# One decoder layer on one core: the last pair's gate products of the pooling branch moved in front of the branch, and three output-projection units issued row by row

## The chip, the cores and the metric

The kernel runs on one core of a Trainium2 chip, as one launch. The time is device microseconds (us) from the launch's start to its end. Every change is judged by the median of several runs; one further execution is recorded by the profiler, and all rows come from such a recorded execution.

## The reference, cut to what matters

The program computes one layer of a decoder trunk for a prompt of 1024 tokens and for 8 samples of 8 new tokens with a paged key/value cache. The part that matters here is the end of the token mixer:

```
z      = h @ w_in                                  # h: 1088 tokens x 1024
p      = z[..., OFF_P:OFF_G]                       # 4 groups of 128 channels
pooled = trailing mean of p over 2/4/8/16 positions, minus p
pool_out = einsum('btgc,gcd->btgd', pooled, pool_w) * pool_scale
gates  = sigmoid(z[..., OFF_G:]).reshape(B, T, 3, 1024)
merged = gates[:, :, 0] * (att      @ w_br_attn)
       + gates[:, :, 1] * (conv_out @ w_br_conv)
       + gates[:, :, 2] * (pool_out @ w_br_pool)
out    = merged @ w_o
x      = layer_norm(ALPHA * x + g1 * out, ln1_g, ln1_b)   # then SwiGLU and a second norm
```

Everything is float32 and has to be accurate, so each product is made of three: every operand is split into a high part that TensorE takes as it is and a low rest, and high*high, low*high and high*low are summed.

## The kernel before, in words

**Layout.** Activations lie transposed: 128 channels on the partitions, T = 1092 tokens (1024 prompt, 64 sample, 4 padding) along the row. `hhi` and `hlo` are the eight channel tiles of the mixer's input h, `ahi`/`alo` the four tiles of a branch's input, `merged` the eight tiles of the gated sum. CH = 364 is a third of T, one PSUM bank.

**Weights** come in 140 units of 128 rows x 1024 floats (one unit holds the group map, half that size). SyncE loads unit u into `raw[u % 3]` (L405); GpSimd splits it by a cast (L611) and a subtraction (L612) into `whi`/`wlo[u % 3]`. GpSimd may begin with unit u once TensorE has begun unit u-2 (semaphore `w_begun`). For the output projection the functions at L698 and L699 do the same into places of their own (`wohi`, `wolo`), so that all eight units stay; the units from the fourth on wait until the last branch product is done.

**TensorE** does a unit as one `gemm` (L1672, L1676, L1678): for each of eight weight blocks three thirds by three products, 72 matmuls of 364 columns. `psA` and `psB` hold three banks each and are used in turn (`GP`). The part that the change touches runs in this order:

- *Pooling filter.* Four units (`U_POOL`) give p of group 3, 2, 1, 0 (`POOL_ORDER`, windows 16, 8, 4, 2). For each, ScalarE copies PSUM to `pb` (L996), TensorE transposes the last 15 and the 64 sample tokens of `pb` for the state outputs (L2012, L2013), VectorE runs the window sums and subtracts (L1414 to L1429, into `yp`), ScalarE casts `yp` to `ahi` (L998), VectorE takes the rest into `alo` (L1433), ScalarE copies the transposed tokens to `ptok` and sends them out (L1002 to L1006).
- *Group maps.* One half unit: per group 9 matmuls. ScalarE scales into `ahi` (L1009), VectorE takes the rest into `alo` (L1437).
- *Third branch,* `branch(2, ...)`: a loop of four turns, one for each pair of channel tiles. A turn is a gate unit into psA, a gate unit into psB (ScalarE takes their sigmoids into `sg`, L967) and a branch unit, half of it into psA, half into psB. VectorE multiplies by the sigmoid (L1343) and adds into `merged` (L1345). The last pair's VectorE work stands apart (L1449 to L1457).
- *Low parts of merged.* ScalarE casts `merged` tile by tile to `hhi` (L1018, the eighth tile in two pieces at L1021), VectorE subtracts into `hlo` (L1444). In VectorE's order tiles 0 to 5 stand ahead of the last pair's product.
- *Output projection.* `wo(c, k)`: column piece c (428, 300 and 364 tokens) of output tile k: eight rows j of three matmuls (L2038, L2041, L2042), each waiting, for the very first, on `hlo` of tile j. The first three use the three banks of psA, the next three those of psB. VectorE's first eviction (L1476) needs the residual x, which ScalarE fetches into `merged` when all of `hlo` is done (L1025) and scales (L1028).

Each engine's program is written out by hand in the order in which it runs; waits on semaphores join them. Nothing is reordered by a scheduler.

Of the kernel before, what the change touches and what calls it, by code (L numbers as in the profile page):

```python
# [25 lines left out]
ALU = mybir.AluOpType  # L26
ACT = mybir.ActivationFunctionType

P = 128
D = 1024  # L30
KD = D // P
# [36 lines left out]
U_F, U_QKV, U_BRA, U_CONV, U_BRC, U_POOL, U_BRP, U_WO, U_FF0, U_FF, U_FFE, U_END = (  # L68
    0, 1, 13, 25, 37, 49, 54, 66, 74, 78, 138, 140)
RING = 3  # L70
# [28 lines left out]
def build(nc, a, out):  # L99
    with ExitStack() as ctx:  # L100
# [8 lines left out]
        class Region:  # L109
# [3 lines left out]
            def __call__(self, name, shape, dt=F32):  # L113
# [101 lines left out]
        S = Region(r_s, r_end - r_s)  # L215
        sg = [S("sg0", [P, T]), S("sg1", [P, T])]
        part = [S("part0", [P, T]), S("part1", [P, T])]

# [20 lines left out]
        s64 = S("s64", [P, 2, NS])  # L239
        S = Region(r_s + 4 * (4 * T + 16), 8 * 8 * P)  # L240
# [154 lines left out]
        def _(sp):  # L395
# [100 lines left out]

            def branch_loads(u0, gate, w, first=0):
                with sp.Fori(first, 4) as i:
# [14 lines left out]
            for j, g in enumerate(POOL_ORDER):  # L513
                wunit(U_POOL + j, (U_POOL + j) % RING, tiles(w_in, OFF_P + g * P))
            sp.wait_ge(s["w_split"], U_POOL + 4 - RING + 1)
            sp.dma_start(raw[(U_POOL + 4) % RING][:, 0:NT, :],
                         a["pool_w"][0].rearrange("g c d -> c g d")).then_inc(raw_in[(U_POOL + 4) % RING], 16)
            branch_loads(U_BRP, 2, a["w_br_pool"][0])
            for j in range(KD):
# [48 lines left out]
        def _(pool):  # L568
# [188 lines left out]
        def _(act):  # L757
# [204 lines left out]
            def gates(j):  # L962
                with act.Fori(0, 4) as i:
                    for x, ps in (("A", psA), ("B", psB)):
                        act.wait_ge(s[f"g{x}"], i + (4 * j + 1))
# [24 lines left out]
            act.wait_ge(s["mB"], 8)  # L990
            for j, g in enumerate(POOL_ORDER):
                act.wait_ge(s["gemm_done"], 1 + j + 1)
                if j:
                    act.wait_ge(s["pf_done"], j)
                    act.wait_ge(s["pt2_tr"], j)
                nc.scalar.copy(c3(pb[:, LEAD:LEAD + T]), cols(GP[j % 2])).then_inc(s["pcopied"], 1)  # L996
                act.wait_ge(s["pf_done"], j + 1)
                nc.scalar.copy(ahi[:, g, :], yp[:, :]).then_inc(s["phi_done"], 1)  # L998
# [117 lines left out]
        def _(dve):  # L1116
# [331 lines left out]
            dve.wait_ge(s["bA"], 12)  # L1448
            link(V.tensor_tensor(c3(part[0][:, :]), cols(GP[0]), c3(sg[0][:, :]), ALU.mult))  # L1449
            V.tensor_tensor(merged[:, KD - 2, :], merged[:, KD - 2, :], part[0][:, :], ALU.add).then_inc(s["mA"], 1)  # L1450
            merged_low(KD - 2, slice(0, T), KD - 1)
            dve.wait_ge(s["bB"], 12)
            for n, (c0, c1) in enumerate(((0, 2), (2, 3))):
                at = slice(c0 * CH, c1 * CH)
                link(V.tensor_tensor(part[1][:, at].rearrange("p (c n) -> p c n", n=CH), psB[:, c0:c1, 0:CH],
                                     sg[1][:, at].rearrange("p (c n) -> p c n", n=CH), ALU.mult))
                V.tensor_tensor(merged[:, KD - 1, at], merged[:, KD - 1, at], part[1][:, at], ALU.add).then_inc(s["mB"], 1)  # L1457
# [199 lines left out]
        def _(pe):  # L1657
# [297 lines left out]
            def branch(j, u0, free_a, free_b, ready):  # L1955

                for first, last in ((0, 1), (1, 4)):
                    with pe.Fori(first, last) as i:
# [19 lines left out]
                        for k, x in enumerate("AB"):  # L1978
                            gemm((u0 + 2) % RING, GP[k], [(2 * t + k, t) for t in range(NT)], ahi, alo, done=s[f"b{x}"],
                                 begin=k == 0, free=((s[f"sg{x}"], i + (4 * j + 1)),))  # L1980
                        if j < 2:
# [18 lines left out]
            branch(1, U_BRC, (s["y_done"], NT), (s["u_done"], NT), ((s["clo_done"], NT),))  # L2000

            for g in range(NT):
# [12 lines left out]
            for j, g in enumerate(POOL_ORDER):  # L2015
                if j >= 2:
                    pe.wait_ge(s["mlo_done"], j - 1)
                pe.wait_ge(s["plo_done"], j + 1)
                gemm((U_POOL + NT) % RING, GP[j % 2], [(g, g)], ahi, alo, done=s["gemm_done"],
                     begin=j == 0)  # L2020
            branch(2, U_BRP, (s["mlo_done"], NT), (s["mlo_done"], NT), ((s["mlo_done"], NT),))

            def wo(c, k):

                n, o = c * KD + k, wo_bank(c * KD + k)
                hi, lo = wo_w[k]
                if c == 0:
                    unit(U_WO + k)
                if n < 6:
                    pe.wait_ge(s["mA" if n < 3 else "mB"], 12 if n < 3 else 13)  # L2030
                else:
                    pe.wait_ge(s["wo_ev"], n - 5 if n < 2 * KD + 6 else 2 * KD + 3 * (n - 5 - 2 * KD) - 1)
                if n == KD:
                    pe.wait_ge(s["hlo_done"], 2 * KD + 1)
                for j in range(KD):
                    if n == 0:
# [5 lines left out]
                    m = mm(o, lo[:, j, :], hhi[:, j, WCOL[c]], start=False, stop=j == KD - 1)  # L2042
                m.then_inc(s["gemm_done"], 1)

# [22 lines left out]

            for k in range(KD):
                wo(0, k)
# [152 lines left out]
```

## Time and profile before

| | |
|---|---|
| median of 3 runs | 2244.74 us (2244.55 to 2249.45) |
| the profiled execution, its own time | 2240.87 us |
| span of its instructions | 2239.3 us |
| granted TensorE clock, mean over the span | 0.966 |
| TensorE matmul busy | 2087.5 us (93%) |
| VectorE / ScalarE / GpSimd busy | 793.1 / 387.1 / 636.6 us |

Times inside the profile are microseconds from the start of the span. A row of the timeline gives the start, the length, the engine, the line of the kernel, the operation, the tiles that it writes and reads, and in square brackets how long the engine had stood idle before it and which instruction ended that. Where equal rows follow one another they are merged and counted (x3). The recorded length of a matmul reaches a little into the next one, so the distance from one start to the next is the better measure: 24 groups of three matmuls make up a unit.

### The profile page before, as it was taken

Reading aid. Unit: us, or ns where it says so; the run is one execution under the profiler, and the core shown is the slowest. Engines: PE = TensorE matmul, PEld = TensorE weight load, DVE = VectorE, ACT = ScalarE, POOL = GpSimd, SP = SyncE. Lnnn points to the kernel's source line nnn. Section 1 sums busy time; section 2 is a strip of 40 time slices with the busy share of each in tenths; the row PEclk is TensorE's granted clock in tenths of the full one; section 3 lists DMA queues with packets and bytes.
Section 4 is the critical chain, followed back from the end, with each engine's and each line's share of the span. In section 5 each row is a group of like instructions: output and inputs, shape, how many; then the busy total and the mean of one; then the engine's idle time right before and its main releaser. Section 6 shows DMA issues by size and latency. Waiting matters only on the chain.

```text
span 2239.3 us, 33058 instructions
## 1 busy us (share of the span) xinstructions
PE 2087.5 (93%) x13046; PEld 1966.5 (88%) x13046; DVE 793.1 (35%) x1423; ACT 387.1 (17%) x700; POOL 636.6 (28%) x482
## 2 busy tenths in 40 slices
PE   4989999788899999999879989899999999999996
PEld 3978887644599999999879989899999999999996
DVE  2444545543200132201622347532334224332326
ACT  2434444412110000000110114400000000000003
POOL 5031111042222322322223334423223323323323
PEclk8989998879999999999989999999999999999998
DMA  9321102067533112222111130011111111111112
GB/s 298 95 80 58 39 29 77 20 227 252 171 98 99 38 38 84 76 76 80 40 39 42 53 127 19 29 48 46 39 47 47 38 47 47 37 47 47 38 38 80
DMA packets 175713, 164.05 MB, mean 73 GB/s; under 512 B 15134, under 2 KB 139506, under 8 KB 175499
## 3 DMA queue, kind: packets, MB, share of 16 engines
q1 hardware_dynamic: 153307, 132.50, 19.3%
q0 software_dynamic: 6144, 17.01, 2.4%
q10 hardware_dynamic: 16184, 13.46, 2.0%
q8 instruction: 54, 0.88, 0.2%
q14 instruction: 24, 0.20, 0.0%
HBM read 149.03 MB, written 14.03 MB: 73 GB/s over the span
## 4 chain that ended last, share of the span: by engine, by line
PE 83%; DVE 7%; issue 2%; SPq 2%; ACT 2%; DMA 2%; POOL 1%; POOLq 0%; ACTq 0%; DVEq 0%
PE psA L1672 11%; PE psA L1678 10%; PE psA L1676 10%; PE psB L1678 9%; PE psB L1676 9%; PE psB L1672 9%; PE psB L1781 2%; PE psB L1784 2%; PE psB L1785 2%; PE psB L1940 2%; PE ps L1850 1%; PE ps L1906 1%; PE psA L1867 1%; DMA kpage<-in_cache_k 1%; DVE hlo L1444 1%
## 5 line engine op out<-in xcount | busy, mean ns | idle before, releaser
L611 POOL CAST whi<-raw 128x1024 fp32r<-128x1024 f32 x131 | 138.7, 1059 | 1208.3 <-PE psA L1672 621.8
L612 POOL TENSOR_TENSOR wlo<-raw,whi 128x1024 fp32r<-128x1024 f32 x131 | 321.3, 2453 | 10.5
L1672 PE MATMUL psA<-hhi,whi 128*128 128x364 f32 x1032 | 230.0, 331 | 11.6 <-DVE yc L1384 7.2
L1678 PE MATMUL psA<-hhi,wlo 128*128 128x364 f32 x1032 | 229.6, 331 | 0.0
L1676 PE MATMUL psA<-hlo,whi 128*128 128x364 f32 x1032 | 229.5, 331 | 0.0
L1678 PE MATMUL psB<-hhi,wlo 128*128 128x364 f32 x936 | 206.8, 329 | 0.0
L1676 PE MATMUL psB<-hlo,whi 128*128 128x364 f32 x936 | 206.7, 329 | 0.0
L1672 PE MATMUL psB<-hhi,whi 128*128 128x364 f32 x936 | 205.8, 328 | 0.0
L1672 PEld LDWEIGHTS psA<-hhi,whi 128*128 128x128 f32 x1032 | 179.8, 190 | 13.6 <-issue 13.5
L1678 PEld LDWEIGHTS psA<-hhi,wlo 128*128 128x128 f32 x1032 | 181.0, 190 | 0.0
L1676 PEld LDWEIGHTS psA<-hlo,whi 128*128 128x128 f32 x1032 | 180.6, 190 | 0.0
L1557 DVE TENSOR_TENSOR ft<-psB,sil 128x1092 f32<-128x1092 f32 x22 | 28.5, 1296 | 405.0 <-PE psB L1678 399.4
L1678 PEld LDWEIGHTS psB<-hhi,wlo 128*128 128x128 f32 x936 | 162.8, 188 | 0.0
L1672 PEld LDWEIGHTS psB<-hhi,whi 128*128 128x128 f32 x936 | 162.3, 188 | 0.0
L1676 PEld LDWEIGHTS psB<-hlo,whi 128*128 128x128 f32 x936 | 162.3, 188 | 0.0
L1083 ACT CAST ahi<-ft 128x1092 fp32r<-128x1092 f32 x22 | 24.3, 1106 | 463.4 <-PE psB L1678 312.5
L1672 PE MATMUL psA<-ahi,whi 128*128 128x364 f32 x366 | 82.4, 334 | 8.5 <-DVE alo L1437 8.5
L1678 PE MATMUL psA<-ahi,wlo 128*128 128x364 f32 x366 | 81.1, 330 | 0.0
L1672 PE MATMUL psB<-ahi,whi 128*128 128x364 f32 x366 | 81.1, 330 | 0.0
L1676 PE MATMUL psA<-alo,whi 128*128 128x364 f32 x366 | 81.1, 330 | 0.0
L1676 PE MATMUL psB<-alo,whi 128*128 128x364 f32 x366 | 81.0, 330 | 0.0
L1678 PE MATMUL psB<-ahi,wlo 128*128 128x364 f32 x366 | 80.8, 329 | 0.0
(412 smaller groups left out, 3665.9 us busy)
## 6 DMA issues: line engine op xcount, KB each, us to landing
raw<-in_w_in SPq DMA_DIRECT2D x53, 512.0 KB, 4.0
raw<-in_w_gate_up SPq DMA_DIRECT2D x44, 512.0 KB, 3.8
kpage<-in_cache_k SPq DMA_DIRECT2D x64, 256.0 KB, 3.7
vpage<-in_cache_v POOLq DMA_DIRECT2D x64, 256.0 KB, 3.9
ada_late<-in_ada_w SPq DMA_DIRECT2D x8, 2048.0 KB, 8.0
raw<-in_w_down SPq DMA_DIRECT2D x22, 512.0 KB, 3.6
ada<-in_ada_w SPq DMA_DIRECT2D x4, 2048.0 KB, 17.2
x_keep<-xt SPq DMA_DIRECT2D x1, 4368.0 KB, 13.8
```

What stands on the lines that cost most here:

```text
L611: link(nc.gpsimd.tensor_copy(whi[slot][:, 0:n, :], raw[slot][:, 0:n, :]))
L612: nc.gpsimd.tensor_tensor(wlo[slot][:, 0:n, :], raw[slot][:, 0:n, :], whi[slot][:, 0:n, :].bitcast(F32), ALU.subtract).then_inc(s["w_split ...
L1083: nc.scalar.copy(to, ft[k][:, :]).then_inc(s["fhi_done"], 1)
L1444: V.tensor_tensor(hlo[:, k, at], merged[:, k, at], hhi[:, k, at].bitcast(F32), ALU.subtract).then_inc(s["hlo_done"], 1)
L1557: V.tensor_tensor(c3(ft[k][:, :]), cols(psB), c3(sil[k][:, :]), ALU.mult).then_inc(s["ft_done"], 1)
L1672: m = mm(ps[:, c, 0:CH], whi[slot][:, b, :], hi[:, k, c * CH:(c + 1) * CH], start=first, stop=False)
L1676: mm(ps[:, c, 0:CH], whi[slot][:, b, :], lo[:, k, c * CH:(c + 1) * CH], start=False, stop=False)
L1678: m = mm(ps[:, c, 0:CH], wlo[slot][:, b, :], hi[:, k, c * CH:(c + 1) * CH], start=False, stop=last)
L1781: m = mm(bank[:, 0:CH], whi[slot][:, k, :], hhi[:, k, at], start=k == 0, stop=False)
L1784: mm(bank[:, 0:CH], whi[slot][:, k, :], hlo[:, k, at], start=False, stop=False)
L1785: m = mm(bank[:, 0:CH], wlo[slot][:, k, :], hhi[:, k, at], start=False, stop=k == KD - 1)
L1940: m = mm(psB[rows, 2, :], ptrs[:, g, rows], vpage[:, half * hpg + g, :], start=g == 0, stop=half == 0 and g == hpg - 1)
```

## The change

The gate units of the third branch's last pair (tiles 6 and 7) are taken out of the branch's loop and stand behind the four pooling units, ahead of the group maps. Their sigmoids go into two tiles of their own, `sgl`, which keep until the end. The loop has three turns, and the last pair's branch unit follows it alone, once the VectorE sums of the third turn have freed psA and psB. TensorE's transposes of one group's tokens, and ScalarE's copies and sends of them, move behind the next unit's product. The output projection's first three units (column piece 0) are issued row by row: rows 0 to 5 of all three, then row 6 of all three, then row 7. The loads and splits of the weight units follow the new order.

```diff
 U_F, U_QKV, U_BRA, U_CONV, U_BRC, U_POOL, U_BRP, U_WO, U_FF0, U_FF, U_FFE, U_END = (
-    0, 1, 13, 25, 37, 49, 54, 66, 74, 78, 138, 140)
+    0, 1, 13, 25, 37, 49, 56, 66, 74, 78, 138, 140)
...
+        S = Region(r_end - 8768, 8768)
+        sgl = [S("sgl0", [P, T]), S("sgl1", [P, T])]
...
+            for j in range(2):
+                wunit(U_POOL + 4 + j, (U_POOL + 4 + j) % RING, tiles(w_in, 3 * 256 + OFF_G + 2 * D + j * P))
+            sp.wait_ge(s["w_split"], U_POOL + 6 - RING + 1)
+            sp.dma_start(raw[(U_POOL + 6) % RING][:, 0:NT, :],
+                         a["pool_w"][0].rearrange("g c d -> c g d")).then_inc(raw_in[(U_POOL + 6) % RING], 16)
+            branch_loads(U_BRP, 2, a["w_br_pool"][0], last=3)
+            wunit(U_BRP + 9, (U_BRP + 9) % RING, tiles(a["w_br_pool"][0], 3 * 256, 256), 4)
...
-            for u_ in range(U_POOL, U_POOL + 4):
+            for u_ in range(U_POOL, U_POOL + 6):
                 one(u_)
-            one(U_POOL + 4, NT)
-            three(U_BRP, 4)
+            one(U_POOL + 6, NT)
+            three(U_BRP, 3)
+            one(U_BRP + 9)
...
             def gates(j):
-                with act.Fori(0, 4) as i:
+                early = j // 2
+                with act.Fori(0, 4 - early) as i:
...
+            for j, g in enumerate(POOL_ORDER):
+                act.wait_ge(s["gemm_done"], 1 + j + 1)
+                if j:
+                    act.wait_ge(s["pf_done"], j)
+                    act.wait_ge(s["pt2_tr"], j)
+                nc.scalar.copy(c3(pb[:, LEAD:LEAD + T]), cols(GP[j % 2])).then_inc(s["pcopied"], 1)
+                if j:
+                    last_rows(j - 1)
+                act.wait_ge(s["pf_done"], j + 1)
+                nc.scalar.copy(ahi[:, g, :], yp[:, :]).then_inc(s["phi_done"], 1)
+            for k, x in enumerate("AB"):
+                act.wait_ge(s[f"g{x}"], 9)
+                nc.scalar.activation(c3(sgl[k][:, :]), cols(GP[k]), ACT.Sigmoid).then_inc(s[f"sg{x}"], 1)
+                if k == 0:
+                    last_rows(NT - 1)
...
-            link(V.tensor_tensor(c3(part[0][:, :]), cols(GP[0]), c3(sg[0][:, :]), ALU.mult))
+            link(V.tensor_tensor(c3(part[0][:, :]), cols(GP[0]), c3(sgl[0][:, :]), ALU.mult))
...
                 gemm(u0 % RING, GP[g % 2], all_k, done=s["gemm_done"])
-                pe.wait_ge(s["pcopied"], g + 1)
                 if g:
-                    pe.wait_ge(s["pt2_copied"], g)
-                tr(mi[0][0:PST, 0:P], pb[:, LEAD + NP - PST:LEAD + NP], ident[:, :])
-                tr(mi[0][0:NS, P:2 * P], pb[:, LEAD + NP:LEAD + TU], ident[:, :]).then_inc(s["pt2_tr"], 1)
-            unit(U_POOL + NT)
+                    last_rows(g - 1)
+            for k, x in enumerate("AB"):
+                u0 = U_POOL + NT + k
+                unit(u0)
+                gemm(u0 % RING, GP[k], all_k, done=s[f"g{x}"], free=((s["pcopied"], NT - 1 + k),))
+                if k == 0:
+                    last_rows(NT - 1)
+            u0 = U_POOL + NT + 2
+            unit(u0)
             for j, g in enumerate(POOL_ORDER):
-                if j >= 2:
-                    pe.wait_ge(s["mlo_done"], j - 1)
+                pe.wait_ge(s["mlo_done"] if j >= 2 else s["sgB" if j else "sgA"], j - 1 if j >= 2 else 9)
                 pe.wait_ge(s["plo_done"], j + 1)
...
             branch(2, U_BRP, (s["mlo_done"], NT), (s["mlo_done"], NT), ((s["mlo_done"], NT),))
-
-            def wo(c, k):
+            unit(U_BRP + 9)
+            for k, x in enumerate("AB"):
+                gemm((U_BRP + 9) % RING, GP[k], [(2 * t + k, t) for t in range(NT)], ahi, alo, done=s[f"b{x}"],
+                     begin=k == 0, free=((s[f"m{x}"], 11),))
+
+            def wo(c, k, js=range(KD)):
...
-                for j in range(KD):
+                for j in js:
...
-            for k in range(KD):
+            for js in (range(KD - 2), range(KD - 2, KD - 1), range(KD - 1, KD)):
+                for k in range(3):
+                    wo(0, k, js)
+            for k in range(3, KD):
                 wo(0, k)
```

ScalarE in the pooling filter, before: from the copy of the first group (window 16) to that of the third.

```order
L996 COPY pb<-psA 128x1092
L998 CAST ahi<-yp 128x1092
L1002 COPY ptok<-ps 15x128
L1003 COPY ptok<-ps 64x128
L1005 DMA out_pool_prompt<-ptok 15x128
L1006 DMA out_pool_sample<-ptok 8x8x128
L996 COPY pb<-psB 128x1092
```

ScalarE, the same place now.

```order
L1017 COPY pb<-psA 128x1092
L1021 CAST ahi<-yp 128x1092
L1017 COPY pb<-psB 128x1092
L1006 COPY ptok<-ps 15x128
L1007 COPY ptok<-ps 64x128
L1009 DMA out_pool_prompt<-ptok 15x128
L1010 DMA out_pool_sample<-ptok 8x8x128
```

The copy that frees PSUM for TensorE stands ahead of the former group's token copies and sends; they stand behind it.

TensorE behind the first pooling unit, before (the last group of its matmuls, the two transposes, the next unit).

```order
L1678 MATMUL psA<-hhi,wlo_56 128x364 x3
L2012 MATMUL ps<-ident,pb 15x128
L2013 MATMUL ps<-ident,pb 64x128
L1672 MATMUL psB<-hhi,whi_54 128x364 x3
L1676 MATMUL psB<-hlo,whi_54 128x364 x3
```

TensorE at the end of the second of the two moved gate units (psB), now, with the first two group maps behind it.

```order
L1698 MATMUL psB<-hhi,wlo_55 128x364 x3
L1692 MATMUL psA<-ahi,whi_53 128x364 x3
L1696 MATMUL psA<-alo,whi_53 128x364 x3
L1698 MATMUL psA<-ahi,wlo_56 128x364 x3
L1692 MATMUL psB<-ahi,whi_53 128x364 x3
L1696 MATMUL psB<-alo,whi_53 128x364 x3
L1698 MATMUL psB<-ahi,wlo_56 128x364 x3
```

Before, each pooling unit was followed at once by transposes that read `pb`; now a whole unit lies between a copy to `pb` and its transposes, and two gate units lie between the pooling units and the group maps.

TensorE in the output projection, before: from row 7 of the first unit to row 0 of the second.

```order
L2038 MATMUL psA<-hhi,whi_52 128x428
L2041 MATMUL psA<-hlo,whi_52 128x428
L2042 MATMUL psA<-hhi,wlo_55 128x428
L2038 MATMUL psA<-hhi,whi_53 128x428
L2041 MATMUL psA<-hlo,whi_53 128x428
L2042 MATMUL psA<-hhi,wlo_56 128x428
```

TensorE, row 6 of the first three units, now (whi_52, whi_53 and wohi_165 are the high parts of unit 1, 2 and 3).

```order
L2074 MATMUL psA<-hhi,whi_52 128x428
L2077 MATMUL psA<-hlo,whi_52 128x428
L2078 MATMUL psA<-hhi,wlo_55 128x428
L2074 MATMUL psA<-hhi,whi_53 128x428
L2077 MATMUL psA<-hlo,whi_53 128x428
L2078 MATMUL psA<-hhi,wlo_56 128x428
L2074 MATMUL psA<-hhi,wohi_165 128x428
L2077 MATMUL psA<-hlo,wohi_165 128x428
L2078 MATMUL psA<-hhi,wolo_166 128x428
```

Row 6 of the first unit is followed by row 6 of the second and third, and before it stand 54 matmuls that need only rows 0 to 5.

## Rows read from the trace of the kernel before

**Rows 1.** The page: the chain that ended last, by engine.

```profile
PE 83%; DVE 7%; issue 2%; SPq 2%; ACT 2%; DMA 2%; POOL 1%; POOLq 0%; ACTq 0%; DVEq 0%
```

**Rows 2.** TensorE's waits, 1060 to 1330 us: released by, total us, times, longest.

```profile
PE psA L1672 <- DVE alo L1437: 11.3, 2, 8.5
PE ps L2012 <- ACT pb L996: 6.6, 4, 3.0
PE psA L2038 <- issue: 6.3, 1, 6.3
PE psA L2038 <- DVE hlo L1444: 4.0, 1, 4.0
```

**Rows 3.** TensorE's timeline from the first pooling unit to the third branch.

```profile
1062.51 0.74 PE L1672 MATMUL psA<-hhi,whi 128*128 128x364 f32 x3
...
1075.97 0.28 PE L2012 MATMUL ps<-ident,pb 128*15 128x128 f32 x1 [1.24 <-ACT pb L996]
...
1091.36 0.28 PE L2012 MATMUL ps<-ident,pb 128*15 128x128 f32 x1 [3.01 <-ACT pb L996]
...
1131.91 1.28 PE L1672 MATMUL psA<-ahi,whi 128*128 128x364 f32 x3 [8.54 <-DVE alo L1437]
...
1139.88 1.25 PE L1672 MATMUL psA<-hhi,whi 128*128 128x364 f32 x3 [2.74 <-DVE alo L1437]
```

**Rows 4.** Two stretches: length, then busy us of each engine, PEclk, DMA share.

```profile
1091.50:1096.00 4.50, 4.50 (x20) 4.50 (x19) 4.36 (x5) 0.00 (x0) 2.55 (x2) 0.62 0.01 1
1292.00:1296.50 4.50, 4.47 (x13) 4.20 (x14) 3.40 (x2) 1.07 (x1) 4.42 (x3) 0.50 0.41 117
```

**Rows 5.** ScalarE's timeline: the psA sigmoids of the third and fourth turn.

```profile
1225.67 1.08 ACT L967 ACTIVATE sg<-psA 128x1092 f32<-128x1092 f32 x1 [22.96 <-PE psA L1678]
...
1261.69 1.08 ACT L967 ACTIVATE sg<-psA 128x1092 f32<-128x1092 f32 x1 [22.96 <-PE psA L1678]
```

**Rows 6.** VectorE's and ScalarE's timelines: first filter's end, last group map's rounding.

```profile
1087.18 0.22 DVE L1429 SCALAR_TENSOR_TENSOR yp<-ps,ps 128x64 f32<-128x64 f32 x1
...
1137.17 1.17 ACT L1009 ACTIVATE ahi<-psB,vecs 128x1092 fp32r<-128x1092 f32 x1 [0.95 <-PE psB L1678]
...
1138.38 1.35 DVE L1437 SCALAR_TENSOR_TENSOR alo<-psB,vecs,ahi 128x1092 fp32r<-128x1092 f32 x1 [0.77 <-ACT ahi L1009]
```

**Rows 7.** TensorE's timeline: the branch's end and the output projection's first three units.

```profile
1285.04 0.66 PE L1678 MATMUL psB<-ahi,wlo 128*128 128x364 f32 x3
1292.03 0.70 PE L2038 MATMUL psA<-hhi,whi 128*128 128x428 f32 x1 [6.33 <-issue]
...
1302.53 0.46 PE L2038 MATMUL psA<-hhi,whi 128*128 128x428 f32 x1 [4.03 <-DVE hlo L1444]
...
1309.42 0.35 PE L2038 MATMUL psA<-hhi,wohi 128*128 128x428 f32 x1
...
1314.08 0.35 PE L2038 MATMUL psB<-hhi,whi 128*128 128x428 f32 x1
```

**Rows 8.** VectorE's timeline at the same place.

```profile
1251.16 3.52 DVE L1345 TENSOR_TENSOR merged<-merged,part 128x1092 f32 x1 [0.15 <-DVE part L1343]
1275.78 12.79 DVE L1444 TENSOR_TENSOR hlo<-merged,hhi 128x1092 fp32r<-128x1092 f32 x6 [21.10 <-ACT hhi L1018]
...
1300.73 4.37 DVE L1444 TENSOR_TENSOR hlo<-merged,hhi 128x728 fp32r<-128x728 f32 x2
```

**Rows 9.** GpSimd's timeline: splits of weight units, alone and beside VectorE.

```profile
1250.01 1.04 POOL L611 CAST whi<-raw 128x1024 fp32r<-128x1024 f32 x1 [8.55 <-PE psA L1672]
1251.14 2.39 POOL L612 TENSOR_TENSOR wlo<-raw,whi 128x1024 fp32r<-128x1024 f32 x1
...
1277.43 2.11 POOL L698 CAST wohi<-raw 128x1024 fp32r<-128x1024 f32 x1
1279.62 3.34 POOL L699 TENSOR_TENSOR wolo<-raw,wohi 128x1024 fp32r<-128x1024 f32 x1
```

**Rows 10.** ScalarE's timeline: the residual's scaling, behind its transfer.

```profile
1313.18 3.07 ACT L1028 ACTIVATE merged<-merged 128x3424 f32<-128x3424 f32 x1 [11.85 <-DMA merged<-x_keep]
```

More of the change, by code:

```diff
@@ L215, in build @@
         S = Region(r_s, r_end - r_s)
-        sg = [S("sg0", [P, T]), S("sg1", [P, T])]
-        part = [S("part0", [P, T]), S("part1", [P, T])]
+        gated = S("gated", [P, 4, T])
+        sg = [gated[:, 0, :], gated[:, 1, :]]
+        part = [gated[:, 2, :], gated[:, 3, :]]
         S = Region(r_s, r_end - r_s)
@@ L239, in build @@
         s64 = S("s64", [P, 2, NS])
-        S = Region(r_s + 4 * (4 * T + 16), 8 * 8 * P)
+        S = Region(r_s + 4 * 4 * T, 8 * 8 * P)
+        assert S.end <= r_end - 8768
         wo_r = [(S("wohi2", [P, 8, P], F32R), S("wolo2", [P, 8, P], F32R))]
@@ L495, in _, with branch_loads @@
             decay_loads(DB - 1)
-            def branch_loads(u0, gate, w, first=0):
-                with sp.Fori(first, 4) as i:
+            def branch_loads(u0, gate, w, first=0, last=4):
+                with sp.Fori(first, last) as i:
                     for j in range(2):
@@ L514, in _ @@
                 wunit(U_POOL + j, (U_POOL + j) % RING, tiles(w_in, OFF_P + g * P))
[L515 to L518, printed above, removed]
+            for j in range(2):
[5 more added lines that the diff above has]
+            wunit(U_BRP + 9, (U_BRP + 9) % RING, tiles(a["w_br_pool"][0], 3 * 256, 256), 4)
             for j in range(KD):
@@ L962, in gates @@
             def gates(j):
-                with act.Fori(0, 4) as i:
+                early = j // 2
+                with act.Fori(0, 4 - early) as i:
                     for x, ps in (("A", psA), ("B", psB)):
-                        act.wait_ge(s[f"g{x}"], i + (4 * j + 1))
+                        act.wait_ge(s[f"g{x}"], i + (4 * j + early + 1))
                         k = "AB".index(x)
@@ L990, in _, with last_rows @@
             act.wait_ge(s["mB"], 8)
[L991 to L998, printed above, removed]
+            def last_rows(j):
+                g = POOL_ORDER[j]
                 act.wait_ge(s["pt2_tr"], j + 1)
@@ L1455, in _ @@
                 link(V.tensor_tensor(part[1][:, at].rearrange("p (c n) -> p c n", n=CH), psB[:, c0:c1, 0:CH],
-                                     sg[1][:, at].rearrange("p (c n) -> p c n", n=CH), ALU.mult))
+                                     sgl[1][:, at].rearrange("p (c n) -> p c n", n=CH), ALU.mult))
                 V.tensor_tensor(merged[:, KD - 1, at], merged[:, KD - 1, at], part[1][:, at], ALU.add).then_inc(s["mB"], 1)
@@ L1955, in branch @@
             def branch(j, u0, free_a, free_b, ready):
-                for first, last in ((0, 1), (1, 4)):
+                early = j // 2
+                for first, last in ((0, 1), (1, 4 - early)):
                     with pe.Fori(first, last) as i:
@@ L1979, in branch @@
                             gemm((u0 + 2) % RING, GP[k], [(2 * t + k, t) for t in range(NT)], ahi, alo, done=s[f"b{x}"],
-                                 begin=k == 0, free=((s[f"sg{x}"], i + (4 * j + 1)),))
+                                 begin=k == 0, free=((s[f"sg{x}"], i + (4 * j + early + 1)),))
                         if j < 2:
@@ L2000, in _, with last_rows @@
             branch(1, U_BRC, (s["y_done"], NT), (s["u_done"], NT), ((s["clo_done"], NT),))
+            def last_rows(g):
+                pe.wait_ge(s["pcopied"], g + 1)
+                if g:
+                    pe.wait_ge(s["pt2_copied"], g)
+                tr(mi[0][0:PST, 0:P], pb[:, LEAD + NP - PST:LEAD + NP], ident[:, :])
+                tr(mi[0][0:NS, P:2 * P], pb[:, LEAD + NP:LEAD + TU], ident[:, :]).then_inc(s["pt2_tr"], 1)
             for g in range(NT):
@@ L2015, in _ @@
+            u0 = U_POOL + NT + 2
+            unit(u0)
             for j, g in enumerate(POOL_ORDER):
-                if j >= 2:
-                    pe.wait_ge(s["mlo_done"], j - 1)
+                pe.wait_ge(s["mlo_done"] if j >= 2 else s["sgB" if j else "sgA"], j - 1 if j >= 2 else 9)
                 pe.wait_ge(s["plo_done"], j + 1)
-                gemm((U_POOL + NT) % RING, GP[j % 2], [(g, g)], ahi, alo, done=s["gemm_done"],
-                     begin=j == 0)
+                gemm(u0 % RING, GP[j % 2], [(g, g)], ahi, alo, done=s["gemm_done"], begin=j == 0)
@@ L2021, in _ @@
             branch(2, U_BRP, (s["mlo_done"], NT), (s["mlo_done"], NT), ((s["mlo_done"], NT),))
-            def wo(c, k):
+            unit(U_BRP + 9)
[3 more added lines that the diff above has]
+            def wo(c, k, js=range(KD)):
                 n, o = c * KD + k, wo_bank(c * KD + k)
                 hi, lo = wo_w[k]
[L2027 to L2032, printed above, removed]
+                if js[0] == 0:
+                    if c == 0:
+                        unit(U_WO + k)
+                    if n < 6:
+                        pe.wait_ge(s["mA" if n < 3 else "mB"], 12 if n < 3 else 13)
+                    else:
+                        pe.wait_ge(s["wo_ev"], n - 5 if n < 2 * KD + 6 else 2 * KD + 3 * (n - 5 - 2 * KD) - 1)
@@ L2042, in wo @@
                     m = mm(o, lo[:, j, :], hhi[:, j, WCOL[c]], start=False, stop=j == KD - 1)
-                m.then_inc(s["gemm_done"], 1)
+                if js[-1] == KD - 1:
+                    m.then_inc(s["gemm_done"], 1)
             def mean(c):
```

## The prediction

> **What bounds the kernel now.** I read the page's chain first: 83% of it is TensorE [rows 1], so a change pays only where TensorE stands idle, or in work that goes away, and none goes away here. The table of TensorE's waits around the change is next [rows 2]: between 1060 and 1330 us it waits 28.2 us in all, 11.3 for the rounded group maps, 6.6 for the copies to `pb`, 6.3 and 4.0 ahead of and inside the first output unit. The timeline places them: 1.24 and 3.01 us behind the first two pooling units (the other two waits share the remaining 2.3), 8.54 between the second and third map, 2.74 ahead of the branch [rows 3], then 6.33 and 4.03 [rows 7]. Last I read the clock behind such waits: it is 0.62 over the 4.5 us from 1091.5 and 0.50 over the 4.5 us from 1292 [rows 4], that is, at or near the 1.2 GHz level where a dense stretch has 2.4. In the first of these stretches 20 matmuls start where a unit's pace of 0.167 us makes 27, so a long wait costs its length and then 1.2 us or more.
>
> **The front: the gate units put into the waits.** One turn of the branch, three units, takes 1261.69 - 1225.67 = 36.02 us [rows 5], so a unit takes 12.01. A map is 9 of a unit's 72 matmuls, 1.50. Before, from the first pooling unit to the branch is 1139.88 - 1062.51 = 77.37 us [rows 3], for four units and four maps (54.0) and 23.3 besides: 17.8 of waits (1.24, 3.01, 2.3, 8.54, 2.74), 0.6 of transposes, and 4.9 left for low clock and handovers.
>
> After, in order:
> - Six units back to back, 72.06. Each pooling unit but the first two waits only for a copy made a unit earlier. Is VectorE in time? Its longest filter (window 16) runs from 1076.0 to 1087.4 [rows 3, 6]; the others do fewer window sums. Walked through with these lengths, with ScalarE's 1.1 us casts and copies, and with GpSimd's splits beside it, the fourth filter's low part is there at about 1120.5, and the maps start at about 1135.5. So the filters have 15 us to spare, and the copy to `pb` of the fourth group 10 us before the second gate unit needs psB.
> - Four pairs of transposes, 0.15 each: 0.6.
> - Four maps, 6.0. The 8.54 us wait inside them goes, since all four low parts are there. What is late next is their rounding. The third map needs psA: from the end of the first map 0.25 to ScalarE, 1.17, then 1.35 on VectorE [rows 6], 2.9 with handovers, of which the second map covers 1.5: a wait of 1.4. The fourth follows at once. The branch waits for the fourth's rounding as now, 2.9 from the end of one to the start of the other (recorded as 2.74 [rows 3]).
>
> The sum is 72.06 + 0.6 + 6.0 + 1.4 + 2.9 = 83.0, with 0.3 for handovers 83.3. The branch loses 24.02 us of gate units. Gain: 77.37 + 24.02 - 83.3 = **18.1 us**. The low clock at 1091.5 and in the third map goes and is in this; that behind the 2.7 us wait ahead of the branch I leave as it is (if it went, 1.2 to 1.5 us more). Queued behind the added waits: behind ScalarE's second `sgl` sigmoid stand the roundings of the maps, which wait for that same stretch of TensorE anyway; behind the transposes' wait for the token copies stands a whole unit, but those copies are some 10 us old by then. SyncE's loads are as many as before, in a new order, each with about 12 us to land; GpSimd splits the two gate units beside the filters, which takes from the 15 us, not from the end.
>
> Bounds of this part: if every wait of [rows 3] up to 8.54 came back except those that two full units must swallow (the second unit fills the 8.54 and its low clock, the first the 3.01), at least 8.54 + 3.01 + some 3.5 of the 4.9 for low clock = 15 is gained; if no low clock follows and the map waits vanish, 18.1 + 1.5 + 1.4 = 21.
>
> **The back: the last product without a gate ahead of it.** Call X the end of the third turn's psA product. Before, the last pair's product ended at B = 1285.54 and the first three output units at 1314.08 [rows 7]: 28.54 us. VectorE had begun the six low parts of `merged` 10 us ahead of B, since two gate units gave it free time. Now it can only begin when the third turn's psB sum is done: the psB product ends at X + 6, VectorE multiplies until X + 7.5 and adds in 3.52, as in each turn [rows 8]: ready at X + 11.1, while TensorE ends the last product at X + 18.0 and stops.
>
> Here VectorE meets GpSimd. A split alone takes 1.04 and 2.39; beside the low parts 2.11 and 3.34 [rows 9], and a low part, 1.28 alone, takes 12.79 / 6 = 2.13 [rows 8]. The extra is what one gets when the two take turns, one whole instruction each: 6 x 1.28 + what GpSimd did meanwhile gives the 12.79. Taking turns in the same way from X + 11.1 (split of the third output unit until X + 15.6, pause until X + 18.2, then five splits in a row), the six low parts end at X + 25.2, psA's last sum at X + 29.9, the seventh low part at X + 34.6, the first piece of the eighth at X + 41.0, all of it at X + 43.8. TensorE starts the output projection at X + 30.0: a wait of 12 us where it was 6.33. Twelve matmuls at low clock in 4.4 us as before (13 touch the 4.5 us of [rows 4]), sixty at 0.194 ((1314.08 - 1309.42) / 24 [rows 7]): row 7 would be reached at X + 44.3, after it is there, so the 4.03 us wait inside the projection and the low clock behind it are gone. End: X + 46.1, 28.0 after the last product. Gain: **0.5 us**: issuing row by row wins back what the later low parts lose. The residual is no new wait: fetched at X + 43.9, 8.0 us, scaling 3.07 [rows 10], first eviction done at X + 56.4; TensorE wants the bank at X + 60.
>
> Bounds: with the low parts as one block of 12.79 and all behind it as before, the end is X + 43.4, gain 3.1; with one more split of GpSimd (2.4 + 1.04) ahead of the last sum, -3. I take the walk, because it reproduces each row of before.
>
> The Trainium skill ("SBUF — State Buffer", "Who interferes with whom") has this as a rule that speaks against the change: a VectorE instruction with two SBUF inputs and a GpSimd instruction that reads SBUF exclude one another for their whole length. The trace agrees (2.13 for 1.28). Without the rule each low part would take 1.28 and the back would gain about 9 us; with it, 0.5.
>
> **Sum.** 18.1 + 0.5 = 18.6 us. Against the profiled execution's 2240.87 that is 2222.3. That execution lies 3.9 under the median of the timed runs, so for the median I take 2244.74 - 18.6, **2226 us**. Everything behind the first three output units (TensorE-bound to the end) moves as a whole.
>
> **The rivals.**
> 1. *The front gains less.* Some of the 1.2 to 3.0 us waits return, because a handover (the copies' `pb` against the transposes, VectorE pushed back by the two extra splits) falls on the path after all, or the back loses 3 and not 0.5. For it: four engines hand over within 12 us units. Against: the slack of 10 to 15 us. Gain 8 to 14: 2231 to 2237, say 2233.
> 2. *More than forecast.* The clock stays up ahead of the branch (1.5) and VectorE wins its turns against GpSimd at the back (2.6): 2244.7 - 22.7 = 2222.
> 3. *The change doesn't do what it says.* The sigmoids are kept, but the filter chain turns out to set the pace, so that the two gate units end where they stood; the waits move behind them. For it: in [rows 6] the first filter takes 11.4 of a unit's 12.0 us. Then only the row-by-row issue counts: 0 to 3, 2243.
> 4. *Slower: the clock.* Mechanism: TensorE stays at 1.2 GHz behind the longer wait at the projection's start (12 us for 6.33) or behind the maps. Price: a matmul of the projection costs 4.4 / 12 = 0.37 there for 0.194, so a unit of 12.0 costs about 10 us more. Against: in the trace the low level ends within 4.5 us each time. It decides once it lasts for 18.6 / 10 = 1.9 units more than before; with three, 2256.
>
> **Chances.** Forecast 0.65 (own range 2222 to 2231), rival 1 0.15, rival 2 0.12, rival 3 0.05, rival 4 0.03. A difference under 0.3%, 6.7 us, can't be told from none here. Faster by more: 0.65 + 0.15 + 0.12 = 0.92; same 0.05 (rival 3); slower 0.03 (rival 4). Range: 2219 to 2233, rival 2 with a point below for the spread of medians, and half of rival 1.
>
> **What would show it.** In the profile after: TensorE's waits for `pb` gone, the wait for the rounded maps 1.2 to 1.4 inside them and 2.7 ahead of the branch, none of 8; the branch's three turns 36.0 each; the first pooling unit to the branch 83 us, not 77; the six low parts begin 7 us ahead of the last product's end and not 10, and take about 14; TensorE waits about 12 us ahead of the output projection and not at all inside its first three units. Wrong would be: any wait over 2 us between the six units, a filter that ends later than 1125, an output projection that starts less than 9 or more than 15 us after the last product, or a wait for the residual.

## The result, and the profile after

| | before | changed |
|---|---|---|
| median, first timing | 2246.23 us (4 runs) | 2222.95 us (4 runs, 2219.02 to 2228.84) |
| ratio, 95% interval | | 0.9898 [0.9876, 0.9919] |
| timed again (label r0_after) | 2245.53 us (23 runs) | 2225.76 us (6 runs) |
| ratio, 95% interval | | 0.9914 [0.9893, 0.9934] |
| profiled execution, its own time / span | 2240.87 / 2239.3 us | 2228.84 / 2226.9 us |

The kernel became faster by 19 to 23 us (by the two ratios; both intervals lie clear of 1); 2226 was forecast. The two profiled spans differ by only 12.4 us, and that is not what the change brings. The first pooling unit of the changed kernel starts at 1066.59 where it started at 1062.51 [rows 3], so this execution was 4.1 us behind before it reached the first changed instruction. When ScalarE squares the first output tile, it is 15.1 us ahead (1332.06 for 1347.13). Between these two points lie 19.2 us. Behind them, where the code is the same, this execution takes 2.7 us longer than the one before. The runs don't show it as a cost of the change: from this squaring to the end the changed kernel takes 894.8 us and the profiled execution of before 892.2, but e8_transposes_only and e2_rows_only, whose code there is that of before, take 893.8 and 894.7.

TensorE's waits from 1050 to 1340 us in the changed kernel (released by, total us, times, longest):

```profile
PE psA L2074 <- issue: 10.8, 1, 10.8
PE psA L1692 <- DVE alo L1457: 4.0, 2, 2.7
```

These two rows take the place of the four of [rows 2]: 14.8 us of waits for 28.2. The waits for the copies to `pb` are gone, the wait inside the first output unit (4.0) is gone, the two waits for rounded maps fell from 11.3 to 4.0, and the wait ahead of the output projection grew from 6.3 to 10.8.

TensorE's timeline over the front:

```profile
1066.59 0.74 PE L1692 MATMUL psA<-hhi,whi 128*128 128x364 f32 x3
...
1090.63 0.27 PE L2028 MATMUL ps<-ident,pb 128*15 128x128 f32 x1
...
1143.86 0.76 PE L1692 MATMUL psA<-ahi,whi 128*128 128x364 f32 x3 [1.23 <-DVE alo L1457]
...
1149.84 0.74 PE L1692 MATMUL psA<-hhi,whi 128*128 128x364 f32 x3 [2.74 <-DVE alo L1457]
```

No bracket stands at the transposes any more: TensorE comes to them a unit later, when the copy that they read has long been made. From the first pooling unit to the branch are 1149.84 - 1066.59 = 83.25 us; two more units of 12.01 lie in it than in the 77.37 of before. Less these it is 59.23: the front gained 18.1.

VectorE at the filter's end and over the back:

```profile
1122.61 1.29 DVE L1453 TENSOR_TENSOR alo<-yp,ahi 128x1092 fp32r<-128x1092 f32 x1 [1.17 <-ACT ahi L1021]
...
1264.64 13.38 DVE L1464 TENSOR_TENSOR hlo<-merged,hhi 128x1092 fp32r<-128x1092 f32 x6
...
1279.26 3.23 DVE L1470 TENSOR_TENSOR merged<-merged,gated 128x1092 f32<-128x1092 f32 x1
...
1291.35 4.40 DVE L1464 TENSOR_TENSOR hlo<-merged,hhi 128x728 fp32r<-128x728 f32 x2
```

GpSimd's timeline beside that sum:

```profile
1278.99 2.34 POOL L707 TENSOR_TENSOR wolo<-raw,wohi 128x1024 fp32r<-128x1024 f32 x1
```

The fourth filter's low part is done at 1123.9, 57.3 us after the first pooling unit's start; the second gate unit ends 72.7 us after it. So VectorE has 15 us to spare. The six low parts take 13.38 us where they took 12.79 [rows 8]. The sum behind them now takes 3.23, where a sum alone takes 1.30 (e4 below): GpSimd's subtraction had begun 0.27 us before it and ran until 1281.33, and the sum ended 1.16 us after that. TensorE at the same place:

```profile
1271.12 0.66 PE L1698 MATMUL psB<-ahi,wlo 128*128 128x364 f32 x3
1282.59 0.70 PE L2074 MATMUL psA<-hhi,whi 128*128 128x428 f32 x1 [10.81 <-issue]
...
1297.26 0.36 PE L2074 MATMUL psA<-hhi,whi 128*128 128x428 f32 x1
...
1299.01 0.35 PE L2074 MATMUL psB<-hhi,whi 128*128 128x428 f32 x1
```

The last product ends at 1271.62, the first three output units at 1299.01: 27.4 us for 28.5 [rows 7]. From the start of the projection it is 16.4 us for 22.05. The wait ahead of it, 4.5 us longer, ate most of what the row order gave. Row 7, reached at 1297.26, had its low part at 1295.75.

The granted clock behind the waits of 2.74 and 10.81 us (a stretch, its length, busy us by engine, then PEclk, where 0.50 is the 1.2 GHz level and 1.00 that of 2.4, and the DMA share):

```profile
1149.80:1154.00 4.20, 4.16 (x17) 4.19 (x18) 0.00 (x0) 0.00 (x0) 3.41 (x2) 0.66 0.02 4
1282.50:1287.50 5.00, 4.92 (x14) 4.63 (x15) 3.85 (x2) 1.10 (x1) 4.92 (x3) 0.50 0.44 119
```

Low clock follows both waits, as it followed those of [rows 4]; that behind the second pooling unit and in the third map is gone.

### The profile page after: what moved, and what is told of

It reads as the page before. It is cut to its first block, busy times and chain, and to the rows that moved or that the text cites. A ratio compares the mean times of both kernels' runs of the same rounds, so it can differ in the third digit from the quotient of the medians.

```text
span 2226.9 us, 33031 instructions
## 1 busy us (share of the span) xinstructions
PE 2084.2 (94%) x13046; PEld 1966.5 (88%) x13046; DVE 794.1 (36%) x1423; ACT 387.1 (17%) x700; POOL 636.0 (29%) x482
## 4 chain that ended last, share of the span: by engine, by line
PE 86%; DVE 5%; issue 2%; SPq 2%; ACT 2%; DMA 2%; POOL 1%; POOLq 0%; ACTq 0%; DVEq 0%
PE psA L1692 11%; PE psA L1698 11%; PE psA L1696 11%; PE psB L1698 10%; PE psB L1696 10%; PE psB L1692 10%; PE psB L1801 2%; PE psB L1804 2%; PE psB L1805 2%; PE psB L1960 2%; PE ps L1870 1%; DMA kpage<-in_cache_k 1%; PE psA L1887 1%; PE ps L1926 1%; PE psA L1889 1%
## 5 line engine op out<-in xcount | busy, mean ns | idle before, releaser
L1577 DVE TENSOR_TENSOR ft<-psB,sil 128x1092 f32<-128x1092 f32 x22 | 28.5, 1296 | 406.0 <-PE psB L1698 399.3
```

Source lines behind the costliest of these rows:

```text
L1577: V.tensor_tensor(c3(ft[k][:, :]), cols(psB), c3(sil[k][:, :]), ALU.mult).then_inc(s["ft_done"], 1)
```

## The experiments

Each was timed beside the kernel before; e4 to e7 share one set of eleven runs of it. "Front" is the stretch from the first pooling unit to the branch, less 24.02 us where two gate units lie in it; "back" is the stretch from the end of the last product to the end of the first three output units. Both are read from TensorE's timeline in one profiled execution of each kernel, as above.

| kernel | front | back | median | ratio to before [95%] |
|---|---|---|---|---|
| before | 77.4 | 28.5 | 2241.45 to 2246.23 | 1 |
| changed (r0_after) | 59.3 | 27.2 | 2225.76 | 0.9914 [0.9893, 0.9934] |
| e1_rows_off | 59.3 | 33.0 | 2231.84 | 0.9938 [0.9914, 0.9963] |
| e2_rows_only | 75.7 | 22.7 | 2240.61 | 0.9971 [0.9957, 0.9986] |
| e3_transposes_back | 66.2 | 27.3 | 2233.82 | 0.9951 [0.9934, 0.9969] |
| e8_transposes_only | 70.2 | 28.5 | 2234.53 | 0.9964 [0.9949, 0.9979] |
| e4_splits_held | as changed | 22.9 | 2217.24 | 0.9880 [0.9860, 0.9901] |
| e5_sum_first | as changed | 20.7 | 2214.51 | 0.9873 [0.9850, 0.9895] |
| e6_sum_first_held6 | as changed | 14.1 | 2210.55 | 0.9850 [0.9828, 0.9872] |
| e7_sum_first_held_all | as changed | 14.1 | 2206.27 | 0.9840 [0.9817, 0.9864] |
| e9_best_again (= e7) | 59.3 | 14.1 | 2210.57 | 0.9848 [0.9822, 0.9875] |

**r0_after.** The changed kernel again.

> The changed kernel itself, timed again beside the kernel before. Theory (the waits went, locally 19 us): ratio to before 0.9915, 19 us less; the 23 us between the first medians is then spread of the runs. Rival (something outside the changed stretch gains 4 us too): 0.9898 again, 23 us less. In the profile: from the first pooling unit to the branch 83.3 us; wait ahead of the output projection 10.8 us; first three output units over 27.4 us after the last product.

The ratio came out as the local gain says, 0.9914, which is 19.3 us. The two ratios' intervals overlap, so the 23 us between the first medians can be spread in part; nothing in the two profiles shows a further 4 us of gain.

**e1_rows_off.** The row order undone.

```diff
-            for js in (range(KD - 2), range(KD - 2, KD - 1), range(KD - 1, KD)):
-                for k in range(3):
-                    wo(0, k, js)
-            for k in range(3, KD):
+            for k in range(KD):
                 wo(0, k)
```

> The changed kernel with the output projection's first three units issued one after the other again. Theory (row 7 is ready some 10.5 us after the start of the projection, and only the row order keeps TensorE busy until then): a wait of 4 us inside the first unit and low clock behind it, 5.6 us slower than the changed kernel, 13.5 us faster than before. Rival (row order is worth nothing, since the low parts set the pace either way): within 1.5 us of the changed kernel.

```profile
1274.28 0.70 PE L2074 MATMUL psA<-hhi,whi 128*128 128x428 f32 x1 [10.79 <-issue]
...
1284.79 0.46 PE L2074 MATMUL psA<-hhi,whi 128*128 128x428 f32 x1 [4.14 <-DVE hlo L1464]
...
1296.35 0.35 PE L2074 MATMUL psB<-hhi,whi 128*128 128x428 f32 x1
```

TensorE's timeline shows the wait inside the first unit back: 4.14 us, and the three units take 22.07 us. The back is 5.6 us longer than in the changed kernel's first profile, the median 6.1 us higher, as the theory said. Against before, with the units in the same order, the back is 4.5 us longer (33.0 for 28.5): that is what the later low parts cost.

**e2_rows_only.** The same edit made to the kernel before, alone.

> The kernel before with nothing but the row-by-row issue of the first three output units. Theory: the 4.03 us wait inside the first unit and the low clock behind it go, the first three units take 16.4 us instead of 22.05: 5.6 us faster than before, 2240. Rival (the low clock lasts longer or a new wait on row 7 comes in): 0 to 3 us faster.

TensorE's waits in this kernel, and its timeline at the end of the three units:

```profile
PE psA L1672 <- DVE alo L1437: 11.3, 2, 8.5
PE ps L2012 <- ACT pb L996: 6.6, 4, 3.0
PE psA L2039 <- issue: 6.3, 1, 6.3
```

```profile
1306.83 0.36 PE L2039 MATMUL psB<-hhi,whi 128*128 128x428 f32 x1
```

The fourth row of [rows 2] is gone, the others stand. The last product ends at 1284.14, so the back is 22.7 us, 5.9 less; the median is 4.9 lower and the ratio says 3 to 10 us. The row order is worth the same 5.6 to 5.9 with and without the rest, and the later low parts cost about the same in this order too: 27.4 in the changed kernel for 22.7 here.

**e3_transposes_back.** The changed kernel with TensorE's transposes right behind each pooling unit.

```diff
                 gemm(u0 % RING, GP[g % 2], all_k, done=s["gemm_done"])
-                if g:
-                    last_rows(g - 1)
+                last_rows(g)
...
-                if k == 0:
-                    last_rows(NT - 1)
```

> The changed kernel with TensorE's transposes of the last tokens right behind each pooling unit again, gate units and row order as changed. Theory (the transposes' wait for the copy to pb is a cost of its own, 1.2 us behind units 1, 3 and 4 and 3 us behind unit 2, with low clock behind the 3 us one): 6 to 9 us slower than the changed kernel, so that moving the transposes makes about 8 of the front's 18 us and the gate units the other 10. Rival (the gate units alone fill the waits, the transposes' place is of no account): within 1.5 us of the changed kernel.

The rows of TensorE's waits that are new:

```profile
PE ps L2028 <- ACT ptok L1007: 5.1, 3, 1.7
...
PE ps L2028 <- ACT pb L1017: 1.2, 1, 1.2
```

The front is 7.0 us longer, the median 8.1 higher: the size was right. The mechanism was right only in part: three of the four waits are for the former group's token copies, which ScalarE now makes behind the copy to `pb`, and no wait is 3 us long. So this kernel isn't the old order but one of its own, with the engines out of step.

**e8_transposes_only.** Therefore also the reverse: the kernel before, with the transposes on TensorE and the token copies on ScalarE moved, and nothing else. TensorE's part of the edit:

```diff
                 gemm(u0 % RING, GP[g % 2], all_k, done=s["gemm_done"])
-                pe.wait_ge(s["pcopied"], g + 1)
                 if g:
-                    pe.wait_ge(s["pt2_copied"], g)
-                tr(mi[0][0:PST, 0:P], pb[:, LEAD + NP - PST:LEAD + NP], ident[:, :])
-                tr(mi[0][0:NS, P:2 * P], pb[:, LEAD + NP:LEAD + TU], ident[:, :]).then_inc(s["pt2_tr"], 1)
+                    last_rows(g - 1)
+            last_rows(NT - 1)
```

> The kernel before with only the transposes of the last tokens (and ScalarE's copies and sends of them) moved behind the next unit's product; the last group's stay behind the fourth unit; gate units and output projection as before. Theory (the waits behind units 1 to 3 hold VectorE's filter chain back, so without them the last filter ends 8 to 9 us earlier and the long wait before the third map stays): the stretch from the first pooling unit to the branch falls from 77.4 to 68 to 70 us, the kernel is 7 to 9 us faster than before, and the gate units' move is worth the other 9 to 10 us. Rival (the four filters on VectorE set the pace, so TensorE only waits later): 0 to 3 us faster.

TensorE's timeline, ahead of the third map and of the branch:

```profile
1121.23 1.28 PE L1679 MATMUL psA<-ahi,whi 128*128 128x364 f32 x3 [8.01 <-DVE alo L1444]
...
1129.44 1.15 PE L1679 MATMUL psA<-hhi,whi 128*128 128x364 f32 x3 [2.74 <-DVE alo L1444]
```

The first pooling unit starts at 1059.22, so the front is 70.2 us, 7.2 less than before; the median is 6.9 lower. Both lie just outside what was expected, and on the side of a smaller gain. The 8 us wait stays. What the gate units do on top is 70.2 - 59.3 = 10.9. Taken in the other order (e3), the gate units alone bring 77.4 - 66.2 = 11.1 and the transposes then 7.0, so the two parts add. Of the 77.4, some 1.6 us are a low clock that another execution of the same code did without (last section). Against that execution's 75.7 the transposes' place brings 5.5 to 7 and the gate units 9.5 to 11.

**e4_splits_held.** The changed kernel; GpSimd takes up the fourth output unit only after the seventh tile's sum.

```diff
             pool.wait_ge(s["bB"], 12)
+            pool.wait_ge(s["mA"], 12)
```

> The changed kernel with GpSimd held: it splits the output projection's fourth to eighth unit only after the seventh tile's sum is done (mA at 12). Theory (VectorE's two-input instructions and GpSimd's splits take turns, one whole instruction each): the low parts end 2 us earlier and the sum after them takes 1.3 for 3.2, so the wait ahead of the output projection falls from 10.8 to about 6.5 and the kernel is 4 to 5 us faster than the changed one. Rival (the low parts take 2.2 us each for another reason, or the later splits come too late for the fourth unit): 0 or slower.

VectorE's low parts and the sum behind them, then TensorE's start of the projection:

```profile
1257.31 10.39 DVE L1465 TENSOR_TENSOR hlo<-merged,hhi 128x1092 fp32r<-128x1092 f32 x6
...
1268.94 1.30 DVE L1471 TENSOR_TENSOR merged<-merged,gated 128x1092 f32<-128x1092 f32 x1
```

```profile
1270.34 0.69 PE L2075 MATMUL psA<-hhi,whi 128*128 128x428 f32 x1 [5.89 <-issue]
```

10.39 us for 13.38, 1.30 for 3.23: together the 4.9 by which TensorE's wait got shorter. Nothing was changed but when GpSimd works, so the stretching of VectorE's instructions is shown to come from it. That the low parts still take 10.39 us and not the 7.31 of e7 fits the third unit's split, which stands ahead of the hold and runs beside the first of them. The median fell by 8.5 us against r0_after, more than the 4.5 of the back; the intervals reach 4 to 5 us to each side of both ratios and leave that open.

**e5_sum_first.** The seventh tile's sum is put behind the first low part, not the sixth, and the three units go row by row from row 0.

```diff
-            for k in range(KD - 2):
-                merged_low(k, slice(0, T), k + 1)
+            merged_low(0, slice(0, T), 1)
             dve.wait_ge(s["bA"], 12)
...
+            for k in range(1, KD - 2):
+                merged_low(k, slice(0, T), k + 1)
...
-            for js in (range(KD - 2), range(KD - 2, KD - 1), range(KD - 1, KD)):
+            for js in (range(j, j + 1) for j in range(KD)):
```

> The changed kernel with VectorE's sum of the seventh tile placed behind the first low part instead of behind the sixth, and the first three output units issued row by row from row 0 on. Theory (the 10.8 us wait is for a bank of psA behind six low parts, not for data): TensorE goes from the last product into the output projection with a wait under 1 us and no low clock, then waits now and then for a row, since GpSimd's splits still stretch the low parts; first three units done 23 us after the last product for 27.4, 4 to 5 us faster than the changed kernel. Rival (the rows' pace on VectorE is the bound, so the sum's place is of no account): within 1.5 us.

```profile
1275.87 0.46 PE L2075 MATMUL psA<-hhi,whi 128*128 128x428 f32 x1 [1.27 <-DVE hlo L1464]
...
1281.91 0.46 PE L2075 MATMUL psA<-hhi,whi 128*128 128x428 f32 x1 [4.01 <-DVE hlo L1464]
...
1284.61 0.56 PE L2075 MATMUL psB<-hhi,whi 128*128 128x428 f32 x1
```

These are TensorE's only waits here; at the start of the projection (1263.90) there is none. So the 10.8 us was a wait for a bank, as the theory says; what is left, 5.3 us, is for late rows. The back is 20.7 us, 2 better than expected. Here too the median fell by more than the back: 11.3 us against r0_after for 6.7. Among themselves e4 to e7, timed beside the same runs of before, follow the stretches more closely: from e4 to e5 the medians fall by 2.7 us for 2.2 in the back, from e5 to e6 and e7 by 4.0 and 8.2 for 6.6.

**e6_sum_first_held6** adds to e5 a hold on GpSimd until six low parts are done, **e7_sum_first_held_all** until all are done.

```diff
             pool.wait_ge(s["bB"], 12)
+            pool.wait_ge(s["hlo_done"], 2 * KD - 2)     # e6;  e7: 2 * KD + 1
```

> As e5, and GpSimd held until the first six low parts are done. Theory: rows come at 1.3 us each, faster than TensorE's 1.75 us for three units' row; first three units done 14 to 17 us after the last product, 10 to 13 us faster than the changed kernel. Rival (the fourth unit's split comes late, or the residual's transfer becomes the wait): 5 to 8 us faster.

> As e5, and GpSimd held until all low parts are done. Theory: no collision at all, but the fourth unit's split ends at about the moment TensorE wants it, so within 2 us of e6 either way. Rival (splits become the bound: five splits of 3.5 us against units of 4.65): no difference, since a split is shorter than a unit.

TensorE in e7: the start of the projection and the end of the three units, then VectorE's low parts 1 to 6 and GpSimd's next split.

```profile
1262.87 0.36 PE L2076 MATMUL psA<-hhi,whi 128*128 128x428 f32 x1
...
1276.94 0.36 PE L2076 MATMUL psB<-hhi,whi 128*128 128x428 f32 x1
```

```profile
1261.40 7.31 DVE L1465 TENSOR_TENSOR hlo<-merged,hhi 128x1092 fp32r<-128x1092 f32 x6
```

```profile
1273.01 1.04 POOL L706 CAST whi<-raw 128x1024 fp32r<-128x1024 f32 x1 [12.69 <-DVE hlo L1465]
```

Six low parts take 7.31 us, 1.22 each. There is no wait and no low clock from the last product on: 14.07 us, which is 72 matmuls at 0.195. The gain over the changed kernel is 13.3 us at this place in both. e6 meets the second half of its rival: its last low parts run beside the splits (4.40 us for the two pieces of tile 8, 1.36 in e7). So the residual is asked for later, its transfer takes longer besides (10.05 us from asking to scaling, 7.5 in e7), and TensorE waits for it once. Why the transfer takes longer no run shows.

```profile
1281.29 0.63 ACTq L1046 DMA_DIRECT2D merged<-x_keep  x1
1291.34 3.07 ACT L1049 ACTIVATE merged<-merged 128x3424 f32<-128x3424 f32 x1 [13.93 <-DMA merged<-x_keep]
```

```profile
1295.35 0.43 PE L2076 MATMUL psA<-hhi,wohi 128*128 128x428 f32 x1 [0.54 <-DVE merged L1498]
```

First ScalarE of e6, then TensorE. That is half a microsecond. The medians of e6 and e7 lie 4.3 us apart where 2 were expected, but the intervals overlap, and e9 with the code of e7 gave a ratio of 0.9848 where e6 gave 0.9850: neither is shown to be the better.

**e9_best_again.** e7 once more.

> The kernel of e7 once more, to pin the best version: ratio to before 0.984 (36 us less) if e7's median holds, 0.986 if the sum of the local gains (19.2 by the change, 13.3 at the projection: 32.5 us) is all there is.

0.9848; both the sum of the local gains (32.5 us, 0.9855) and e7's first ratio lie inside its interval. The best version measured is thus 31 to 38 us faster than before, by medians of 2206 and 2211, where the change alone gives 19.

## Why the prediction was right, point by point

- *Unit of 12.01, six back to back.* Right: the transposes stand at 1090.63, 24.04 us after the start, with no bracket.
- *VectorE in time.* Right: the fourth low part is done 57.3 us after the start, forecast 58.0 (1120.5 - 1062.5).
- *The three turns of 36.0.* Right: the psA sigmoids stand at 1163.65, 1199.68 and 1235.70.
- *The maps' waits, 1.4 and 2.9.* Recorded 1.23 and 2.74, where 1.2 to 1.4 and 2.7 were named.
- *Front 83.3, gain 18.1.* 83.25 and 18.1. That the low clock behind the wait ahead of the branch would stay was left in doubt and came true: 0.66, and 0.62 before (1139.85 to 1144.05 us). The gain has some luck in it: about 1.6 of the 18.1 us are a low clock behind the 3.01 us wait, which the profiled execution of before had and e2_rows_only, same code and same wait, had not. The prediction's step that such a wait costs "its length and then 1.2 us or more" does not hold each time. Which part of the change does it was not in the prediction: e3 and e8 give 7 us to the transposes' new place and 11 to the gate units. The bound "at least 15" was argued from gate units that swallow the waits by themselves. e3 (gain 11.1 at the front) lies below it: with the transposes in their old place waits of 1.2 to 1.7 us come back behind all four pooling units.
- *The back, 0.5.* Measured 1.1. Forecast and measured, in us after the last product: sum of the seventh tile 11.9 and 10.9, end 28.0 and 27.4. The walk by turns gave the six low parts 14.1 us where they took 13.38. That no wait comes back inside the first three units was a near thing in the forecast (row 7 there 0.5 us before it is wanted); it was 1.5. The step itself, that VectorE's later start under GpSimd's splits takes back what the rows give, is shown from three sides: e1 and e2 (the rows are worth 5.6 to 5.9, the later low parts cost 4.5 to 4.7), e4 (GpSimd's splits cost 4.5), e5 (the wait is for the bank behind the low parts). The Trainium skill ("SBUF — State Buffer", "Who interferes with whom") has the rule that a VectorE instruction with two SBUF inputs and a GpSimd instruction that reads SBUF exclude one another. e4 and e7 agree with it: a low part takes 1.22 where GpSimd is held (e7), 2.23 where not.
- *Rival 3, row order alone 0 to 3 us.* Undersized: what the row order removes is the 4.03 us wait and the low clock behind it, 5.9 measured in e2. In the forecast itself that term stood right.
- *Rival 4, the clock.* Not seen: behind the 10.8 us wait the low clock ended after 4.8 us of work, behind the 6.3 us one after 4.5.
- *The residual is no wait.* Right here: its scaling starts at 1303.75 and takes 3.07, and TensorE needs the bank three units of 4.65 behind 1299.01, at 1313 (worked out from these rows). In e6, where the projection starts earlier and the last low parts are slowed by splits, TensorE waits for it 0.54 us; in e7 it does not.
- *Sum.* 18.6 forecast, 19.2 in the profiles. The median, 2223 or 2226, is in the range either way.

## What to carry to other kernels

Work that doesn't depend on a slow chain belongs in that chain's waits. But every short instruction of the waiting engine that reads the chain's result has to be moved too, or the wait comes back there: here some 7 of 18 us were the transposes' place alone. Moving work forward also takes away the cover that it gave where it stood; ask what ran under it (here six low parts) and whose turn it meets now. And of a wait for a buffer, ask what stands ahead of the instruction that frees it: putting one sum ahead of five low parts that TensorE did not need yet, and holding the splits back for 10 us, was worth 13 us, where the whole change brought 19.

## What the runs showed that I had not expected

The same wait doesn't always bring the low clock. Behind the 3.01 us wait after the second pooling unit the kernel before ran at 0.62 [rows 4]; the same code in e2_rows_only, behind the same wait, ran at full clock:

```profile
1091.70:1096.00 4.30, 4.26 (x27) 4.26 (x28) 4.11 (x4) 0.00 (x0) 2.56 (x2) 1.00 0.00 0
```

27 matmuls start in 4.3 us there, 20 in 4.5 before. The third pooling unit and the wait behind it, from one pair of transposes to the next, took 13.54 us there (1091.74 to 1105.28) and 15.10 before (1091.36 to 1106.46). These 1.56 us are nearly all of the difference between the 75.7 us of e2's unchanged front and 77.4.

The runs of one kernel spread widely (before: 2235.9 to 2254.98), and where profiles show it, the spread lies ahead of the changed code. The changed kernel's two profiled executions differ by 12.9 us in span, and 12.6 of these are there at the first pooling unit (1066.59 and 1054.00). In the ten other profiled executions that unit starts between these two times. For the runs without a profile this is not shown. In the samples' attention, from 430 to 620 us, the changed kernel's two executions differ in the clock; first the one of the first timing, then that of r0_after:

```profile
430.00:620.00 190.00, 157.75 (x910) 99.08 (x911) 65.24 (x180) 37.76 (x77) 58.31 (x85) 0.88 0.62 197
```

```profile
430.00:620.00 190.00, 156.93 (x1008) 99.97 (x1009) 62.64 (x173) 37.16 (x75) 60.28 (x86) 0.95 0.62 197
```

The mean clock is 0.88 in one and 0.95 in the other. Many short waits of TensorE lie there; that more of them were followed by the low level in the first is likely from these rows, but not counted. What decides it is not settled by these runs. For a change of 5 us the local stretches say more than the medians.
